# Small constants of a two-layer encoder kernel: laid out by DMA through a scratch in memory instead of by small TensorE products

## The reference

```python
for i in range(DEPTH):                                  # DEPTH = 2
    h = rms_norm(x, norm_g[i])
    proj = h @ w_in[i]
    (a_u, a_v, a_z, b_x, b_z, c_q, c_kv, c_kr, c_z, d_q, d_k, d_v, d_z, gates) = split(proj)
    y_a = (spatial_gating(a_u, a_v, ln_v_g[i], ln_v_b[i], sgu_w[i], sgu_b[i]) * silu(a_z)) @ w_a_out[i]
    y_b = (multiscale_pool(b_x, pool_w[i], pool_scale[i]) * silu(b_z)) @ w_b_out[i]
    y_c = (latent_attention(c_q, c_kv, c_kr, positions, ..., q_norm_g[i], k_norm_g[i]) * silu(c_z)) @ w_c_out[i]
    y_d = (stick_breaking_attention(d_q, d_k, d_v) * silu(d_z)) @ w_d_out[i]
    merged = sum of sigmoid(gates) * (y_a, y_b, y_c, y_d)
    x = x + merged @ w_o[i]
    x = x + sigmoid(rms_norm(x, ple_norm_g[i]) @ w_ple_gate[i]) * (p[i] @ w_ple[i])
```

## Time and profile before

| | |
|---|---|
| median of 3 runs | 1361.28 us (1361.24 to 1361.36) |
| profiled execution, span from first to last instruction | 1359.3 us |
| TensorE matmul busy (PE) | 1352.9 us, 100% |
| TensorE weight load busy (PEld) | 1137.5 us, 84% |
| VectorE busy (DVE) | 693.2 us, 51% |
| ScalarE busy (ACT) | 561.1 us, 41% |
| GpSimd busy (POOL) | 605.7 us, 45% |
| DMA moved | 126.32 MB, mean 93 GB/s |

### The profile page before, as it was taken

The page is one execution under the profiler, slowest core; times in us unless marked ns, Lnnn a source line. Parts: engine busy times, 40 slices in busy tenths (PEclk is TensorE's granted clock), DMA queues, the critical chain, the costliest instruction groups (busy, mean ns, idle before and its releaser), DMA issues.

```text
span 1359.3 us, 16179 instructions
## 1 busy us (share of the span) xinstructions
PE 1352.9 (100%) x6417; PEld 1137.5 (84%) x6417; DVE 693.2 (51%) x1063; ACT 561.1 (41%) x870; POOL 605.7 (45%) x455
## 2 busy tenths in 40 slices
PE   9999999999999999999999999999999999999998
PEld 8888888888888888888888888888888888888887
DVE  7996445145553223274769955451445432343743
ACT  6365454255542222224444554443555322222242
POOL 3544252444344454454554542434333444544543
PEclk9999999999999999999999999999999999999999
DMA  7322222222222332333333222223222223323322
GB/s 207 94 86 94 63 82 74 93 80 91 78 78 93 102 99 94 108 101 98 96 101 94 85 94 62 78 70 101 78 78 81 90 94 107 95 93 110 105 97 93
DMA packets 68268, 126.32 MB, mean 93 GB/s; under 512 B 9040, under 2 KB 37984, under 8 KB 68192
## 3 DMA queue, kind: packets, MB, share of 16 engines
q1 hardware_dynamic: 66960, 124.72, 29.5%
q10 hardware_dynamic: 1232, 0.55, 0.1%
HBM read 123.15 MB, written 2.10 MB: 92 GB/s over the span
## 4 chain that ended last, share of the span: by engine, by line
PE 98%; DMA 1%; ACT 1%; DVE 0%; POOL 0%; SPq 0%; issue 0%
PE ps L491 31%; PE ps L493 31%; PE ps L492 31%; PE ps L773 1%; PE ps L708 1%; PE ps L809 1%; PE ps L695 1%; PE ps L541 0%; DMA x<-x_in 0%; PE ps L556 0%; PE ps L551 0%; DMA par<-par_in 0%; ACT w_hi L981 0%; PE ps L627 0%; SPq L397 0%; POOL w_lo L466 0%
## 5 line engine op out<-in xcount | busy, mean ns | idle before, releaser
L464 POOL TENSOR_TENSOR w_lo<-w_raw,w_hi 128x512 fp32r<-128x512 f32 x222 | 304.2, 1370 | 729.4 <-ACT w_hi L981 729.2
L491 PE MATMUL ps<-h_hi,w_hi 128*128 128x512 f32 (+1 forms) x1160 | 452.6, 390 | 0.0
L493 PE MATMUL ps<-h_hi,w_lo 128*128 128x512 f32 (+1 forms) x1160 | 450.2, 388 | 0.0
L492 PE MATMUL ps<-h_lo,w_hi 128*128 128x512 f32 (+1 forms) x1160 | 450.0, 388 | 0.0
L981 ACT ACTIVATE w_hi<-w_raw 128x1024 fp32r<-128x1024 f32 x227 | 238.6, 1054 | 174.3 <-PE ps L493 169.6
L466 POOL TENSOR_TENSOR w_lo<-w_raw,w_hi 128x512 fp32r<-128x512 f32 x222 | 304.2, 1370 | 0.0
L491 PEld LDWEIGHTS ps<-h_hi,w_hi 128*128 128x128 f32 x1160 | 217.9, 188 | 45.2 <-DVE h_lo L1342 1.0
L493 PEld LDWEIGHTS ps<-h_hi,w_lo 128*128 128x128 f32 x1160 | 217.8, 188 | 45.0
L492 PEld LDWEIGHTS ps<-h_lo,w_hi 128*128 128x128 f32 x1160 | 217.9, 188 | 43.4
L1778 DVE SCALAR_TENSOR_TENSOR m_part<-th,ps 128x512 f32<-128x512 f32 x48 | 33.0, 687 | 237.9 <-PE ps L493 237.7
L1207 ACT ACTIVATE th<-ps 128x512 f32<-128x512 f32 x48 | 28.7, 597 | 183.5 <-PE ps L493 183.5
(11 more groups left out here) (330 smaller groups left out, 1989.0 us busy)
## 6 DMA issues: line engine op xcount, KB each, us to landing
w_raw<-w_in SPq DMA_DIRECT2D x180, 512.0 KB, 3.5
w_raw<-w_in SPq DMA_DIRECT2D x92, 128.0 KB, 2.5
w_raw<-w_in SPq DMA_DIRECT2D x36, 256.0 KB, 3.0
x<-x_in SPq DMA_DIRECT2D x8, 256.0 KB, 5.1
w_raw<-w_in SPq DMA_DIRECT2D x32, 64.0 KB, 2.1
out_x<-x SPq DMA_DIRECT2D x7, 256.0 KB, 3.9
p_raw<-p_in SPq DMA_DIRECT2D x2, 512.0 KB, 4.5
w_raw<-w_in ACTq DMA_DIRECT2D x4, 128.0 KB, 2.8
```

The costliest lines, as they stand in the source:

```text
L464: pool.tensor_tensor(w_lo_t[s][:, 0:4, :], w_raw_t[s][:, 0:4, :], w_hi_t[s][:, 0:4, :].bitcast(F32), ALU.subtract)
L491: pe.matmul(o, a_hi, b_hi, start=first, stop=False, skip_group_check=skip)
L492: pe.matmul(o, a_hi, b_lo, start=False, stop=False, skip_group_check=skip)
L493: return pe.matmul(o, a_lo, b_hi, start=False, stop=last, skip_group_check=skip)
```

## The change

The two rotary weight vectors of both layers and the frequencies are copied element by element into one row of 288 values in memory (`table_row`: 4 x 64 + 32), by five DMAs. Behind chunk av1 SP waits for them and loads the row into every partition (`table`, 128 x 288). `ln_col` is loaded straight into `small` with an access pattern that puts 8 single values into each partition. The five TensorE instructions, the VectorE instructions that fed or copied them, and their semaphores go; the readers take slices of `table`.

```diff
+FREQ_AT = 2 * DEPTH * ROPE
+TABLE = FREQ_AT + HALF
...
+        table_row = nc.dram_tensor("table_row", (TABLE,), F32).ap()
+        def gain_of(l, u):
+            o = (2 * l + u) * ROPE
+            return table[:, o:o + ROPE].rearrange("p (a c) -> p a c", a=2)
...
             load(0, "av0")
-            sync.dma_start(freq[:], const_in[:, CC["inv_win"].start:CONSTS]).then_inc(pos_loaded, 16)
+            for l in range(DEPTH):
+                for u, name in enumerate(("qr", "kr")):
+                    c, o = l * PARAMS + PC[name].start, (2 * l + u) * ROPE
+                    sync.dma_start(table_row[o:o + ROPE].rearrange("(p u) -> p u", u=1), par_in[0:ROPE, c:c + 1],
+                                   allow_slow_non_contiguous=True).then_inc(row_stored, 16)
+            sync.dma_start(table_row[FREQ_AT:TABLE].rearrange("(p u) -> p u", u=1), const_in[0:HALF, CC["freq"]],
+                           allow_slow_non_contiguous=True).then_inc(row_stored, 16)
...
-                        sync.dma_start(ln_t[0:2 * G, :], rows_in[l, 0:2].rearrange("u (g p) -> (u g) p", p=P)).then_inc(
-                            rows_loaded, 16)
+                        sync.dma_start(sm("ln_col"), rows_in[l, 0:2].rearrange("u (g p) -> p (u g)", p=P),
+                                       allow_slow_non_contiguous=True).then_inc(rows_loaded, 16)
...
                         load(l, name)
+                    if l == 0 and name == "av1":
+                        sync.wait_ge(row_stored, 16 * (2 * DEPTH + 1))
+                        sync.dma_start(table[:], table_row.partition_broadcast(P)).then_inc(table_loaded, 16)
...
-                    if rope_frequencies and u:
-                        pe.wait_ge(freq_made, after(0))
-                        pe.wait_ge(lat_taken, after(0))
-                        pe.transpose(ps[:, FREQ_AT:FREQ_AT + P], freq_b[:], ident[:]).then_inc(freq_ready, 1)
...
-            def rope_rows(l):
-                pe.wait_ge(gain_diag, after(l))
-                if l == 0:
-                    pe.wait_ge(freq_taken, after(0))
-                pe.wait_ge(rows_loaded, (l + 1) * 32)
-                pe.transpose(ps[:, 2 * 512 + P:2 * 512 + P + 2 * G], ln_t[0:2 * G, :], ident[0:2 * G, 0:2 * G])
-                pe.matmul(bank(2, P), ones[:], gain_d[:], start=True, stop=True).then_inc(gain_ready, 1)
...
-                pe.wait_ge(gain_taken, after(l))
...
-            def gain_rows(l):
-                dve.tensor_scalar(gain_d[:, 0:ROPE], ident[:, 0:ROPE], col(l, "qr"), None, ALU.mult)
-                dve.tensor_scalar(gain_d[:, ROPE:P], ident[:, 0:ROPE], col(l, "kr"), None, ALU.mult).then_inc(
-                    gain_diag, 1)
+            def pool_gains(l):
...
-                    dve.tensor_scalar(freq_b[:], ones[:], freq[:, G:G + 1], None, ALU.mult).then_inc(freq_made, 1)
...
-                    dve.wait_ge(freq_ready, after(0))
-                    dve.tensor_copy(freq_row[:], ps[:, FREQ_AT:FREQ_AT + HALF]).then_inc(freq_taken, 1)
-                    dve.wait_ge(freq_taken, after(0))
+                    dve.wait_ge(pos_loaded, 16 * TB)
+                    dve.wait_ge(table_loaded, 16)
                     rope_angles()
...
-                    if k == 3:
-                        dve.wait_ge(gain_ready, after(l))
-                        dve.tensor_copy(sm("ln_col"), ps[:, 2 * 512 + P:2 * 512 + P + 2 * G])
-                        dve.tensor_copy(gain_row[:].rearrange("p q a c -> p (q a c)"), bank(2, P)).then_inc(
-                            gain_taken, 1)
```

More of the change, by code:

```diff
@@ L148, in build @@
         cs_tok = sb("cs_tok", [P, TB, 2, HALF])
-        gain_row = sb("gain_row", [P, 2, 2, HALF])
+        table = sb("table", [P, TABLE])
         q_cos = sb("q_cos", [P, TB, 2, HALF])
@@ L154, in build @@
         eps = sb("eps", [P, 1])
-        gain_d = sb("gain_d", [P, 2 * ROPE])
         ring_at = (nc.sbuf_base - P + 255) // 256 * 256 + P
@@ L190, in build @@
             ("ckvn_lo", [SEQ], F32R))
-        vn_hi, vn_lo, rows, mix_off, ln_t = plan(
+        vn_hi, vn_lo, rows, mix_off = plan(
             36, 58, ("vn_hi", [TB, SEQ], F32R), ("vn_lo", [TB, SEQ], F32R), ("rows", [SEQ], F32),
-            ("mix_off", [G, P], F32), ("ln_t", [P], F32))
+            ("mix_off", [G, P], F32))
         lat_t, krs, r_b, n_t, xh = plan(
@@ L202, in build @@
         (krr,) = plan(83, 84, ("krr", [TB, 2, HALF], F32))
-        pos_i, pos_f, freq = plan(22, 23, ("pos_i", [TB], I32), ("pos_f", [TB], F32), ("freq", [G + 1], F32))
-        ang, turns, freq_b = plan(22.5, 24, ("ang", [TB, HALF], F32), ("turns", [TB, HALF], F32), ("freq_b", [P], F32))
-        (freq_row,) = plan(21.5, 22, ("freq_row", [HALF], F32))
+        pos_i, pos_f = plan(22, 23, ("pos_i", [TB], I32), ("pos_f", [TB], F32))
+        ang, turns = plan(22.5, 24, ("ang", [TB, HALF], F32), ("turns", [TB, HALF], F32))
         (c_st,) = plan(16, 20, ("c_st", [CONSTS], F32))
@@ L257, in sems @@
             return [sem(n) for n in names.split()]
+        table_row = nc.dram_tensor("table_row", (TABLE,), F32).ap()
+        def gain_of(l, u):
+            o = (2 * l + u) * ROPE
+            return table[:, o:o + ROPE].rearrange("p (a c) -> p a c", a=2)
         x_loaded = [sem(f"x_loaded{d}") for d in range(KD)]
-        pos_loaded, par_loaded, const_loaded, rows_loaded, p_loaded, out_stored = sems(
-            "pos_loaded par_loaded const_loaded rows_loaded p_loaded out_stored")
+        pos_loaded, par_loaded, const_loaded, rows_loaded, p_loaded, out_stored, row_stored, table_loaded = sems(
+            "pos_loaded par_loaded const_loaded rows_loaded p_loaded out_stored row_stored table_loaded")
         first_hi_made, first_lo_made, last_half = sems("first_hi_made first_lo_made last_half")
@@ L501, in project, with project_rows @@
                 last.then_inc(done(l, name), 1)
-            def project_rows(l, name, i, hi, lo, b, n=SEQ, rope_frequencies=False):
+            def project_rows(l, name, i, hi, lo, b, n=SEQ):
                 w_hi, w_lo = chunk(l, name)
@@ L604, in front @@
                 project_rows(l, "av0", 0, hx_hi, hx_lo, 4)
-                project_rows(l, "av1", 1, hx_hi, hx_lo, 4, rope_frequencies=l == 0)
+                project_rows(l, "av1", 1, hx_hi, hx_lo, 4)
                 pe.wait_ge(n_diag, after(l))
@@ L610, in front @@
                 project_rows(l, "av2", 2, hx_hi, hx_lo, 4)
-                rope_rows(l)
                 project_rows(l, "av3", 3, hx_hi, hx_lo, 4)
                 pe.wait_ge(rb_made, after(l))
-                pe.wait_ge(gain_taken, after(l))
                 for i in (3, 2, 1, 0):
@@ L1379, in rope_angles @@
                 full = [P, TB, HALF]
-                settle(dve.tensor_tensor(ang[:], over(pos_f[:], full, 2), over(freq_row[:], full, 1), ALU.mult))
+                settle(dve.tensor_tensor(ang[:], over(pos_f[:], full, 2), over(table[:, FREQ_AT:TABLE], full, 1), ALU.mult))
                 settle(dve.tensor_scalar(turns[:], ang[:], float(1 / (2 * np.pi)), ROUND, ALU.mult, ALU.add))
@@ L1421, in front @@
                     constants_taken()
[L1422 to L1424 removed]
+                    pool_gains(0)
                 dve.wait_ge(n_root, after(l))
@@ L1530, in rope_tables @@
                     full, part = [P, TB, 2, HALF], [P, TB, HALF]
-                    dve.tensor_tensor(q_cos[:], over(cos, full, 2), over(gain_row[:, 0], full, 1), ALU.mult)
-                    dve.tensor_tensor(q_sin[:, :, 0, :], sin, over(gain_row[:, 0, 0], part, 1), ALU.mult)
-                    dve.scalar_tensor_tensor(q_sin[:, :, 1, :], sin, -1.0, over(gain_row[:, 0, 1], part, 1), ALU.mult,
+                    dve.tensor_tensor(q_cos[:], over(cos, full, 2), over(gain_of(l, 0), full, 1), ALU.mult)
+                    dve.tensor_tensor(q_sin[:, :, 0, :], sin, over(gain_of(l, 0)[:, 0], part, 1), ALU.mult)
+                    dve.scalar_tensor_tensor(q_sin[:, :, 1, :], sin, -1.0, over(gain_of(l, 0)[:, 1], part, 1), ALU.mult,
                                              ALU.mult)
-                    settle(dve.tensor_tensor(krs[:], krs[:], over(gain_row[:, 1], full, 1), ALU.mult))
+                    settle(dve.tensor_tensor(krs[:], krs[:], over(gain_of(l, 1), full, 1), ALU.mult))
                     dve.tensor_tensor(krr[:], krs[:], over(cos, full, 2), ALU.mult)
@@ L1827, in tail @@
                 if l + 1 < DEPTH:
-                    gain_rows(l + 1)
+                    pool_gains(l + 1)
                 def weighed(d):
```

9 lines of the change are left out of this document (2 added, 7 removed).

## The result

The changed kernel takes 1363.87 us (median of 12 runs, 1363.43 to 1365.64) against 1361.05 for the kernel before on the same chip (12 runs, 1360.43 to 1361.45): ratio 1.0024, 95% interval 1.0016 to 1.0031. The forecast of 1360.8 and its range to 1361.9 are wrong.

What follows compares the result with a forecast made beforehand. TensorE was taken as the bound (98% of the chain), waiting at bx3 for VectorE's `h` tiles. Span 1359.3 - 0.48 = 1358.8, + 2.0 = 1360.8 us, other terms costing nothing; range 1359.8 to 1361.9.

Steps and rivals of the forecast that it cites:

- the one on SP's queue: SP's added issues and transfers: av1 issued 1.9 us later, av2 1.2 later, `row_stored` by 21.2 to 21.7, cost 0.
- Free too: Av1 at ScalarE, 1.9 us later: 1.1 taken from idle time before `lat_sq`, 0.8 from the 2.0 slack; no cost.
- the prediction's own sign of being wrong: At VectorE's `h` chain: idle time before `n_t` of 0 and a chain starting after 40.6 would show it wrong.
- the small form of rival 3: Rope angles run against GpSimd's `w_lo` and end 0.5 to 1 us late: 1361.3 to 1361.8 us; chance 0.10.
- Rival 3: Single elements hold the DMA queue before av2, TensorE waits at bx3: slower; chance 0.10 small form, 0.05 for 1363 and more.
- heavy form: `row_stored` takes 10 us, av2 lands at 34.7, TensorE waits at bx3: 1363.1 us, 1368 at 15 us; chance 0.05.
- The factor of 19 for rearranged patterns: Skill page's penalty on `ln_col`'s DMA: 23 us for the transfer, about 20 us slower; given little weight.
- The `ln_col` transfer is hidden: DMA of 1024 single elements before av2: 1.2 us, upper end 3.3 with `table` and `rows`, all hidden, cost 0.
- The TensorE work: Five instructions removed from TensorE: 1.38 us together, reaching bx3 0.77 earlier in layer 0 and 0.61 in layer 1.
- The two copies together: VectorE's `ln_col` and `gain_row` copies inside the `h` chain: removing them gains 0.16 us in each layer.
- "nothing" for `gain_d` in layer 1: Removing VectorE's `gain_d` instructions: gain 0, as in layer 1 they precede work that waits for TensorE's gate products.
- my 0.48: Total gain at bx3: 0.32 us in layer 0 plus 0.16 in layer 1; the other 0.90 turns into waiting.

Runs made afterwards that it cites:

- x3: The changed kernel with its five stores made from contiguous memory, contiguous on both sides, at the same place in SP's program: 1361.23 us (before: 1360.92).
- y2: The changed kernel with its five stores described element by element from a contiguous row of `const_in`; the elements were joined: 1360.87 us (before: 1360.77).
- w3: The changed kernel with the stored elements 16 bytes apart and the table loaded from a row of `const_in`: 1361.26 us (before: 1360.57).
- z1: The changed kernel with the stored elements 512 bytes apart and the table loaded from a row of `const_in`: 1361.27 us (before: 1360.98).
- w2: The changed kernel with the stored elements 64 bytes apart and the table loaded from a row of `const_in`: 1361.07 us (before: 1360.57).
- x1: The kernel before with `ln_col` alone loaded by DMA, its TensorE transpose and VectorE copy gone: 1360.90 us (before: 1360.92).
- y3: The changed kernel without stores: the caller lays out the table as an input and puts the layer norm columns into `par`: 1359.95 us (before: 1360.77).
- z3: The changed kernel with gathers into an SBUF row behind av1, one contiguous store behind av2, broadcast behind av3: 1359.69 us (before: 1360.98).
- y4: The kernel before with VectorE's copies `ln_col` and `gain_row` moved behind the `h` chain: 1360.49 us (before: 1360.77).
- w4: z3 with VectorE's two `gain_d` products of layer 1 put back, their result unread: 1360.09 us (before: 1360.57).
- y1: The changed kernel with the five transfers gathering into SBUF instead of memory, the table loaded from a row of `const_in`: 1361.26 us (before: 1360.77).
- x2: The changed kernel with `ln_col` as before (`ln_t` transposed by TensorE, copied by VectorE): 1363.18 us (before: 1360.92).
- z2: The changed kernel with the five stores taking their elements from the copy of `par` in SBUF: 1363.04 us (before: 1360.98).

## Why the prediction was wrong

**The step that failed** is the one on SP's queue: "four more are 4 x 0.47 = 1.9 us in front of the `pos_i`, `c_st` and av1 loads", stores that land by "21.2 to 21.7", and from them "Free too". The trace shows the prediction's own sign of being wrong: no idle time before `n_t` and a chain that starts after 40.6. Two terms of the step were mis-sized:

- Issue: five stores take 0.59 to 0.62 us each, and the queue then holds SP up for another 1.1 to 1.7 us (at `pos_i` in x3, at `c_st` in y2 and the changed kernel). Av1 is issued 3.8 to 4.5 us late, not 1.9. In x3 and y2 that puts ScalarE back by 3.0 to 3.6; 1.1 is absorbed ahead of `lat_sq` as forecast, and `pos_f` starts only 0.2 late in y2 (36.76 against 36.55). But the angles then run into GpSimd's `w_lo` and take 3.2 us longer, and `n_t` starts 2.55 late (43.14 against 40.59). Its first pair is shorter (1.41 against 3.10), so the first `h_lo` is 0.97 us late (44.59 against 43.62); the copies that are gone leave 0.84 of it at the last one (54.93 against 54.09), the +0.85 of the table. Against the -0.32 without stores this costs 1.2. It is the small form of rival 3, and it eats the gain.
- Landing: 5.3 us in the median for four of the stores and 7.5 for the fifth, so at 25.55 and not at 21.2 to 21.7. And, what the step had no term for, the transfers behind them are held too: `c_st` lands after 8.1 us instead of 3.3, 6.6 without the longer issue. That brings ScalarE from about 27.5 to 30.5 and the end of bx3 from +0.85 to +3.91. I took `out_x` and `pos_i` as the nearest rows. Neither is a store of touching single elements, and this is what matters: the same elements stored 16 bytes apart landed in 3.1 us (w3).

Rival 3 named the kind (single elements hold the queue, angles late, waits at bx3), with 0.05 for its heavy form, but put it in front of av2 behind a 10 us wait for `row_stored`. That wait was 0.8 us. The hold came earlier, in front of av1, where I had only counted issues. The Trainium skill, "DMA: Bandwidth & Descriptors", section Specifications, says that a transfer under 512 bytes makes the engine read, modify and write. That rule alone would have charged z1, w2 and w3 as much as the changed kernel; they show that the small size isn't enough. The factor of 19 for rearranged patterns (same page, section Rules for kernel authors), which I gave little, isn't seen for gathers into SBUF: x1 measures no difference.

**What held.** The `ln_col` transfer is hidden (x1). The TensorE work is 0.77 us up to bx3 in layer 0 and 0.68 in layer 1 by the table (y3); of it 0.32 comes through in layer 0, as forecast (y3, z3), and the rest becomes a wait for `h_lo`: 1.9 us on the loader, the number that the forecast gave. The two copies together are worth 0.14 to 0.15 us per layer (y4). Layer 1 keeps 0.23 (forecast 0.16). In the changed kernel itself layer 1 gains the same 0.23.

**What was missing** on the other side: "nothing" for `gain_d` in layer 1. Its two instructions (0.33 us) stand ahead of the last products of layer 0. Without them the turns of VectorE and GpSimd fall otherwise there, and TensorE's wait for `w_lo` at the start of layer 1 goes from 0.77 to 0.24 (w4 brings it back). Without the stores the change is worth 0.32 + 0.56 + 0.23 = 1.1 us (z3), twice my 0.48.

**Open:** why touching elements hold the engines. That each of 16 engines writes into a piece of memory that others write too would fit; whether it is that, or neighbours on one engine, wasn't tried. Nor is it known whether 8 bytes apart would do, and why SP's issues are held wasn't followed: they are in y1 too, which stores nothing to memory.

## What to carry over

Before a layout is moved to DMA, look at both ends of each element: gathers of single elements into SBUF were free here, also where the elements touch, while 288 elements stored side by side to memory held the transfers behind them for several us. Put helper transfers behind the loads that an engine is about to wait for, gather in SBUF and store once. Where two engines share SBUF by turns, the slack in front of a chain isn't what the trace shows as idle: three instructions that slipped beside GpSimd's took 1.2 to 1.3 us instead of 0.2 to 0.3.

## Not expected of the hardware

- Behind five stores of 64 or 32 single elements, 4 bytes apart, the next large load took 8.1 us to land, 6.8 in x2 and 6.6 in z2; with the elements 16 bytes apart it took 3.2, as without them.
- The elements' own packets show nothing of it: between 21 and 22 us 389 packets made up a busy share of 0.20. The held time is first seen in `c_st`'s packets, 1.86 us each.
- SP's issue of a 64-element transfer takes 0.6 us against 0.47 for a load of weights, and behind five such issues SP took longer over the next ones (`pos_i` 3.5 us for four in x3 and 3.2 in y1, 1.9 before).
